# Query units in two token halves, an earlier search of the half tile, and gathered rows moved between stages of a product-key expert layer

## What is computed

```python
q = (tb @ w_q).reshape(PEER_BLOCK, PEER_HEADS, 2, PEER_HALF)      # 1024 -> 8 heads x 2 x 128
s = einsum('thik,hink->thin', q, sub_keys)                        # 128 keys per head and half
s_top, i_top = top_k(s, 16)
cand = s_top[:, :, 0, :, None] + s_top[:, :, 1, None, :]
best_s, best_c = top_k(cand.reshape(..., 256), 16)
eid = i1 * N_KEYS + i2                                            # one of 16384 experts
g = softmax(best_s)
act = gelu(einsum('thkd,td->thk', u_tab[eid], tb))
x = x + einsum('thkd,td', g * act, v_tab[eid])
```

## Time and profile before

| | us |
|---|---|
| median of 3 runs | 2277.96 |
| lowest and highest | 2274.05, 2281.59 |
| the profiled execution | 2277.83 |
| its span | 2276.1 |
| TensorE busy in it | 2229.8 (98%) |
| VectorE busy | 1585.5 (70%) |
| ScalarE busy | 814.1 (36%) |
| GpSimd busy | 1475.2 (65%) |

### The profile page before, as it was taken

The page is one execution under the profiler, slowest core; times in us unless marked ns, Lnnn a source line. Parts: engine busy times, 40 slices in busy tenths (PEclk is TensorE's granted clock), DMA queues, the critical chain, the costliest instruction groups (busy, mean ns, idle before and its releaser), DMA issues.

```text
span 2276.1 us, 38281 instructions
## 1 busy us (share of the span) xinstructions
PE 2229.8 (98%) x14510; PEld 2152.9 (95%) x14510; DVE 1585.5 (70%) x2800; ACT 814.1 (36%) x1201; POOL 1475.2 (65%) x851
## 2 busy tenths in 40 slices
PE   8999999999999999999999999999989999999998
PEld 8999999997799999999999999999989999999998
DVE  7866444546678336768978889898478777777774
ACT  4443223432133002133433344444344444444442
POOL 5554333432354555557878887889778888888873
PEclk9999999999999999999999999999999999999999
DMA  6224323225763233248888897999999999999982
GB/s 215 84 80 137 97 92 101 93 96 194 250 230 128 84 126 94 84 132 275 304 286 289 291 313 248 300 331 318 355 364 396 374 369 374 385 370 375 381 311 79
DMA packets 212800, 535.19 MB, mean 235 GB/s; under 512 B 16816, under 2 KB 101168, under 8 KB 210224
## 3 DMA queue, kind: packets, MB, share of 16 engines
q1 hardware_dynamic: 111392, 234.65, 31.7%
q0 software_dynamic: 46080, 167.79, 19.7%
q10 hardware_dynamic: 55184, 130.77, 15.7%
HBM read 453.89 MB, written 79.25 MB: 234 GB/s over the span
## 4 chain that ended last, share of the span: by engine, by line
PE 85%; DVE 7%; POOL 2%; DMA 2%; ACT 1%; issue 1%; ACTq 0%; DVEq 0%; SPq 0%; POOLq 0%
PE ps L1008 47%; PE ps L732 30%; PE ps L1066 2%; POOL w_lo L706 1%; DVE prev L1875 1%; PE ps L909 1%; DMA gbuf<-gate_scratch 1%; POOL ug L698 1%; PE ps L896 1%; PE ps L904 1%; PE ps L1021 1%; PE ps L913 1%; PE ps L929 1%; DVE n_lo L1991 1%; DVE oh L2097 1%
## 5 line engine op out<-in xcount | busy, mean ns | idle before, releaser
L673 POOL TENSOR_SCALAR w_hi<-raw 128x1024 fp32r<-128x1024 f32 x129 | 139.5, 1081 | 516.3 <-issue 384.0
L706 POOL TENSOR_TENSOR w_lo<-raw,e_hi 128x1024 fp32r<-128x1024 f32 x128 | 326.4, 2550 | 95.2 <-PE ps L1008 85.3
L706 POOL TENSOR_TENSOR w_lo<-raw,w_hi 128x1024 fp32r<-128x1024 f32 x128 | 318.9, 2492 | 86.6 <-PE ps L1008 84.5
L1008 PE MATMUL ps<-p_hi,w_lo 128*128 128x416 f32 x1024 | 361.4, 353 | 0.0
L1008 PE MATMUL ps<-g_hi,w_lo 128*128 128x416 f32 x1024 | 359.6, 351 | 0.0
L675 POOL TENSOR_TENSOR w_lo<-raw,w_hi 128x1024 fp32r<-128x1024 f32 x129 | 320.7, 2486 | 10.8
L732 PE MATMUL ps<-h_hi,w_hi 128*128 128x288 f32 (+2 forms) x1216 | 273.0, 306 | 1.6 <-ACT ma L1342 1.6
L732 PE MATMUL ps<-h_lo,w_hi 128*128 128x288 f32 (+2 forms) x1216 | 262.1, 297 | 0.0
L732 PE MATMUL ps<-h_hi,w_lo 128*128 128x288 f32 (+2 forms) x1216 | 261.7, 296 | 0.0
L2075 DVE CUSTOM_DVE_ANT_0 ug<-ug,ps 128x1024 f32<-128x1024 f32 x160 | 192.3, 1213 | 72.2 <-DMA ug<-rows_u,eid 56.4
L698 POOL DMA_INDIRECT ug<-rows_u,eid x160 | 214.8, 1342 | 37.5 <-issue 24.3
(11 more groups left out here) (358 smaller groups left out, 5086.0 us busy)
## 6 DMA issues: line engine op xcount, KB each, us to landing
raw<-units SPq DMA_DIRECT2D x385, 512.0 KB
gate_scratch<-gt SPq DMA_DIRECT2D x52, 512.0 KB
activation_scratch<-ge ACTq DMA_DIRECT2D x120, 208.0 KB
abuf<-activation_scratch ACTq DMA_DIRECT2D x30, 832.0 KB
gbuf<-gate_scratch ACTq DMA_DIRECT2D x30, 832.0 KB
prev<-ssm_in ACTq DMA_DIRECT2D x8, 1024.0 KB, 6.7
ssm_s<-prev ACTq DMA_DIRECT2D x8, 1024.0 KB, 4.5
cxb<-parked_tiles ACTq DMA_DIRECT2D x8, 870.0 KB, 6.8
```

What stands on the lines that cost most here:

```text
L673: pool.tensor_scalar(w_hi[:, s, :], raw[:, r, :], 1.0, 1.0, ALU.mult, ALU.mult).then_inc(s_whi, 1)
L706: pool.tensor_tensor(w_lo[:, n % 2, :], raw[:, n % RAW, :], e_hi[m % HS_].bitcast(F32), ALU.subtract)\
L1008: last = mm(accp[par], w[:, k * P:(k + 1) * P], x_[:, k, t0:t0 + ND], start=k == 0 and i == 0, stop=k == KT - 1 and i == 2)
```

## The change

- The query projection runs as 32 half units (N_HALF): the 16 weight units are streamed twice, first for tokens 288 to 575, then for tokens 0 to 287. High parts come from ScalarE and low parts from GpSimd, as for expert units; half units count as m = -32 to -1. Q_RAW becomes 8 half units.
- The first tile (128 gathered tokens) is searched in two parts of four heads, with scores before half units 10 and 17. The half tile's scores come before half unit 19, and it is searched second, from m = -5; the full tiles follow at 6, 28 and 50 instead of 4, 24 and 44.
- The first seven gathers stand behind the low parts of m = -13, -11, ... -1 instead of units 2, 3 and 4.
- Dots beside searches: 14 in the half tile and 38 in each full tile, all 128, instead of 26, 26, 26 and 12. Beside gate blocks, from the third on, 24 of the 32 spread dots, instead of 38 of the 128; the turned rows for them lie in PSUM banks 2 and 3. The last 8 spread dots come one a unit from unit 120 on; before, 32 stood there, 9 of them ahead of the gates.
- VectorE makes the wider sum `g_spread` ahead of the first gate block, not in the half tile's search. The gates of the first block start at unit 74 instead of 76.

```diff
-TT = [(T_ROWS, PH)] + [(t, PH) for t in range(0, T_HALF, P)] + [(T_HALF, PH // 2)]
+TT = [(T_ROWS, PH), (T_HALF, PH // 2)] + [(t, PH) for t in range(0, T_HALF, P)]
+DENSE = [j for j, (t, _) in enumerate(TT) if t < ND]
-PAIR = 2
+PAIR = 4
-UT = [4, 20, 20, 20, 10]
-M_TILE = [sum(UT[:j]) for j in range(len(UT) + 1)]
+M_TILE = [None, -5, 6, 28, 50, 72]
+UT = [0] + [b - a for a, b in zip(M_TILE[1:], M_TILE[2:])]
-UG_FIRST = [3, 2, 2]
-M_FIRST = 2
+M_FIRST = -13
+UG_FIRST = [1, 0, 1, 0, 1, 0, 1, 0, 1, 0, 1, 0, 1]
-DOTS_T = [0, 26, 26, 26, 12]
+DOTS_T = [0, 14, 38, 38, 38]
+N_BESIDE = 24
+B_SPREAD = 2
+DOTS_B = [0] * B_SPREAD + [(b + 1) * N_BESIDE // (NB - B_SPREAD) - b * N_BESIDE // (NB - B_SPREAD)
+                           for b in range(NB - B_SPREAD)]
+N_TAIL = N_PICK + N_BESIDE
-DOTS_U = [9, 0, 0, 1, 1, 1, 1, 1, 1]
-DOTS_V = [2, 2, 2, 2, 2, 2, 3, 2]
+DOTS_U = [0, 1, 1, 1, 1, 1, 1, 1, 1]
+DOTS_V = [0, 0, 0, 0, 0, 0, 0, 0]
-Q_RAW = 4
+Q_RAW = 8
+N_HALF = 2 * N_WQ
+U_PEER = U_WQ + N_HALF
...
-            for m in range(2 * NKEYS):
+            for m in range(-N_HALF, 2 * NKEYS):
                 n = U_PEER + m
-                pool.wait_ge(s_ehi, m + 1)
+                pool.wait_ge(s_ehi, N_HALF + m + 1)
                 pool.wait_ge(s_unit, n - 1)
...
+            query_half(0, gu, parts=s_u, ready=KT)
+            added_squares(1 + GROUPS)
+            query_half(1, gu, (0, 2))
+            last_squares(1 + GROUPS)
+            query_half(1, gu, (2, KT))
+            query_half(2, gu, (0, 4))
+            spread_out(1 + GROUPS)
+            query_half(2, gu, (4, KT))
+            for j in range(3, Q_RAW):
+                query_half(j, gu)
+            query_half(Q_RAW, (g_hi, g_lo), parts=s_h, ready=KT)
+            for j in range(Q_RAW + 1, N_HALF):
+                if j == Q_RAW + 2:
+                    first_scores(0)
+                elif j == Q_RAW + 4:
+                    turn_rows(0, g_sum[:], h_rows)
+                elif j == N_WQ + 1:
+                    first_scores(1)
+                elif j == N_WQ + 3:
+                    pe.wait_ge(s_scs, 1)
+                    scores(1)
+                query_half(j, (g_hi, g_lo))
...
+                if b == B_SPREAD - 1:
+                    pe.wait_ge(s_ud, N_PICK)
+                    turn_rows(1, spread_columns, h_beside)
...
+            for j in range(Q_RAW, N_HALF):
+                half = slice(HK, TK) if j < N_WQ else slice(0, HK)
+                link(query_copy(j, q[:, j % N_WQ, half]))
+                act.sem_inc(s_accf[(U_WQ - L_SHIFT + j) % 2], 1)
+                act.sem_inc(s_q, 1)
+                if j == N_HALF - HS_:
+                    act.wait_ge(s_qs, Q_RAW)
+                expert_hi(j + HS_ - N_HALF)
+                if j == Q_RAW + 2:
+                    first_scores_out(0)
+                elif j == N_WQ + 1:
+                    first_scores_out(1)
+                elif j == N_WQ + 2:
+                    first_exp(0)
+                elif j == N_WQ + 4:
+                    scores_out(1)
+                elif j == N_WQ + 9:
+                    first_exp(1)
```

More of the change, by code:

```diff
@@ L131, in dots_of, with turned_by @@
     return range(d0, d0 + DOTS_B[b])
-N_TURNED = len(TT) - 1 if ND > T_HALF else len(TT) - 2
+def turned_by(j):
+    return sum(i <= j for i in DENSE)
 def store_after(B, i):
@@ L965, in _, with expert_part, expert_unit, query_half @@
                 tile(U_WO + j, L_WO + j, m_hi, m_lo)
[L966 to L979, removed]
+            gu = (gu_hi, gu_lo)
+            L0 = U_PEER - L_SHIFT
+            def expert_part(m, c, half, out, mov, columns, ks=(0, KT), parts=None, ready=0):
+                par = (L0 + c) % 2
+                if ks[0] == 0:
+                    pe.wait_ge(s_w, U_PEER + 1 + m)
+                    pe.wait_ge(s_accf[par], half)
+                hi, lo = e_hi[c], w_lo[:, (U_PEER + c) % 2, :]
+                for k in range(*ks):
+                    if parts:
+                        pe.wait_ge(parts, ready + k + 1)
+                    for i, (w, x_) in enumerate(((hi, mov[0]), (hi, mov[1]), (lo, mov[0]))):
+                        last = mm(out, w[:, k * P:(k + 1) * P], x_[:, k, columns],
+                                  start=k == 0 and i == 0, stop=k == KT - 1 and i == 2)
+                if ks[1] == KT:
+                    last.then_inc(s_unit, 1)
+            def expert_unit(m, c, half, mov, t0, parts=None):
+                expert_part(m, c, half, accp[(L0 + c) % 2], mov, slice(t0, t0 + ND), parts=parts)
+            def query_half(j, mov, ks=(0, KT), parts=None, ready=0):
+                m = j - N_HALF
+                t0 = HK if j < N_WQ else 0
+                expert_part(m, m % HS_, (L0 + m) // 2, queried(j), mov, slice(t0, t0 + HK), ks, parts, ready)
             def first_scores(c):
@@ L2074, in row_dot @@
                 rows = row_landed(k)
-                dve.tensor_tensor_reduce(rows, rows, h_rows if k < N_PICK else h_spread, 1.0, 0.0, ALU.mult, ALU.add, dots[:, k:k + 1])\
+                dve.tensor_tensor_reduce(rows, rows, h_rows if k < N_PICK else h_beside if k < N_TAIL else h_spread, 1.0, 0.0, ALU.mult, ALU.add, dots[:, k:k + 1])\
                     .then_inc(s_ud, 1)
@@ L2190, in step @@
                         row_dot(due.pop(0))
-                search(PARTS + j, 0, heads, step, j - 1)
+                search(PARTS + j, 0, heads, step, turned_by(j - 1))
                 dve.sem_inc(s_pk, 1)
@@ L2334, in inputs_of @@
     units[U_WO:U_WQ] = tiles(A(w_o)[0])
-    units[U_WQ:U_PEER] = tiles(A(peer_w_q)[0])
+    units[U_WQ:U_WQ + N_WQ] = units[U_WQ + N_WQ:U_PEER] = tiles(A(peer_w_q)[0])
     uu = A(peer_u)[0].reshape(NKEYS, NKEYS, KT, P).transpose(1, 3, 2, 0).reshape(NG, GI, P, D)
```

201 lines of the change are left out of this document (91 added, 110 removed).

## The result

Measured: 2295.9 us, median of five runs (2294.1 to 2300.6), against 2278.4 us of the kernel before (2274.1 to 2281.8, five runs on the same chip). By the medians the change made the kernel 17.5 us slower. The ratio over all these runs is 1.0085, 95% interval 1.0073 to 1.0096, which is 19.4 us (17 to 22). The profiled execution took 2295.7 us, so its sum can be set against the 2277.8 of the one before.

The account below looks back on a forecast made before the run. TensorE was taken to bound the kernel, so only its waits could be won; terms 0.9 + 1.6 + 2.4 + 2.6 + 4.4 - 1.5 - 6.3 = +4.1 on 2277.8 gave 2281.9 us, range 2268 to 2296.

Parts of the forecast that it names:

- rival C: Tiles among expert units: GpSimd 96% full cannot catch up, each full search costs 6.6 us; 2290.3 us, chance 0.20.
- Step 1: Start of the query stage: fewer matmuls stand before the spreading of the inverse root, +1.6 us.
- Step 3: Query stage's second search: its comparison holds GpSimd's low parts and gathers beside half units, +2.6 us.
- The eight transposes: One more turning of rows, priced within the query projection, +0.9 us.
- Step 2: Near half unit 20: TensorE waits for a low part queued behind the gather that needs four heads' ids, +2.4 us.
- Step 5: Ends of the three full searches: late dots 5.4 us, then lock 3.0 each; 11.4 against 9.6 before, +1.8 us.
- Step 4: Expert units: bursts of four gathers behind units 0 and 37, +1.1 us each, and the half tile, +0.4.
- The gate blocks: 24 gathers instead of 38 there, so TensorE loses less to late low parts, -1.5 us.
- the turning: One more turning of rows as eight transposes, expected with the query projection, +0.9 us.
- Step 6: Last units before the outputs: fewer gathers precede the second group's gates' load, 12 us instead of 16.73; -6.3 us with clock.
- A: Searches among expert units: long steps fall between low parts and cost nothing; 2269.2 us, faster, chance 0.20.
- B: Last units: they give nothing back, the gates' loads take 16.7 us again; 2288.2 us, chance 0.16.

Follow-up runs that it names:

- e_mix: Changed kernel with comparison and product of the four later searches in halves, due dots taken between the halves; 2287.2 us, ratio 1.0042 to the kernel before.
- e_fill2: Changed kernel with unused matmuls filling TensorE's waits in the query stage and among expert units, also ahead of units 28 and 73; 2292.9 us, ratio 1.0063.
- e_nolock: Changed kernel with comparison and product of the three full searches replaced by instructions with one SBUF input; 2292.2 us, ratio 1.0055.
- e_tail: Changed kernel with no spread dot beside the gate blocks, all 32 at the end as in the kernel before; 2305.8 us, ratio 1.0118.
- e_even: Changed kernel with 32 dots a full tile instead of 38, the 18 others beside the first nine gate blocks; 2295.2 us, ratio 1.0065.
- b_split4: Kernel before with the searches among expert units cut in quarters, dots left where they were; 2276.8 us, ratio 0.9989.
- e_mix3: Changed kernel with quarters and dots between in the first two full searches, halves without dots between in the last; 2288.2 us, ratio 1.0045.
- b_mix4: Kernel before with comparison, product and sum of searches among expert units in quarters, due dots between; 2270.0 us, ratio 0.9954.

## Why the prediction was wrong, point by point

The forecast was 2281.9; it missed by 14.0 us. The direction was right. The measured time lies at the very top of the stated range, 2296, which was there for rival C. Of the miss 8.0 us are steps 4 and 5, 3.7 steps 1 to 3, and 3.9 lie ahead of the change; the rest takes some 2 off. Its own steps:

**Step 1** was too small. It took the spreading of the inverse root to stay where it was, 13.1 us after the stage's start, with 12 matmuls fewer before it. The spreading came after 15.4 us, and the missing matmuls still had to be done: 2.3 + 1.6 = +3.9 for +1.6. TensorE had waited 1.57 us in half unit 0 and then stood at 0.51 of its clock from 900 to 907 us. In e_mix, where the same wait was not followed by half clock, the spreading came after 12.3 us, and the step is worth +0.8. So half clock, which the step left out, made 3.1 of the 3.9.

**Step 3** held: the second search cost 2.8 us at half units 26 and 27, for +2.6. The eight transposes took 0.8, but among the gate blocks. What the sum left out in the stage's favour is a wait of 0.87 us for ScalarE at its end in the kernel before, which is gone.

**Step 2** had the wait right in its place (half unit 20, behind the gather that waits for its ids) and 0.9 short in size, 3.3 for 2.4. It left out what follows the wait, half clock from 978.7, worth 1.6.

**Step 5 failed**, and it is the largest part. It priced the three search ends at 11.4 us, 5.4 with late dots in the first tile and 3.0 of lock in each other. The waits came to 11.1 us, the stretches to 17.7: 6.8, 5.9 and 5.0. What is missing is the half clock behind each wait, 6.1 us, which the sum carried for the last units and nowhere else, though the earlier trace rows showed 0.91 at the middle search end of the kernel before. By e_fill2 half of those 6.1 would have been lost to the next wait anyway. That the waits agree with the 11.4 is in part luck. In the first tile the step had late dots hold unit 28 for 5.4 us; what came was 3.88 at unit 26, from a gather held by the comparison, which had to be out of the way before the late dots showed (e_nolock: 4.13). In the other two the lock held 4.05 and 3.19, for 3.0 each. And "nine slots let VectorE run 5 us ahead, which covers it" was not so: with the lock gone, e_nolock waited 2.86 us for dots in the second tile.

**Step 4** gave +1.1 for a burst of four gathers: 1.5 behind unit 37, nothing behind unit 0. The half tile's 0.4 was measured as 0.4.

**The gate blocks** gave -2.6 without the turning, for -1.5. The two waits of the kernel before (1.04 and 0.78 us) are gone. By e_tail 24 gathers cost nothing there, by e_even 18 more cost 0.31 us each. Ahead of them stood a wait that no step had: unit 73, 2.0 us, behind a gather of 3.01 and a low part of 3.70 us beside the one-hots of the first block, which now fall on a full tile's last gathers.

**Step 6** held in place and size: the first three output units took 6.8 us less (17.5 for 24.4), the gates' load 11.4 for 12, with 3 gathers in the 30 us ahead of it instead of 12. That the fewer gathers are the cause fits these rows and was not shown: e_tail, made for it, lost its time elsewhere.

**The unchanged stage**: 3.9 us of the 17.5 between the two executions lie ahead of the change, 2.9 of them in one stretch of half clock at 558.7. It stood in 7 of 17 profiled executions of the study, b_split4's among them, whose code is the kernel before's there. So it can come without the change. But that the change has no part in it is not shown: 13 of the 14 executions with the changed query stage had such a stretch somewhere between 530 and 620 us, and 1 of 3 of the kernel before and its two variants. The interval over all runs, 17 to 22 us, is the better measure of the whole, and how much of it these stretches make was not settled.

**The rivals.** A fell: each full search cost time. B fell: the gates' load took 11.4 us, not 16.7. C is not settled. Its 6.6 us a search end are near the measured 5.9 on average, in part for another reason (the clock), and the lighter load of e_even took 3.6 and 2.5 us off the first two ends and nothing off the third. None had the clock.

**What the change costs once the search ends are eased in both**: e_mix3 against b_mix4, by the two ratios 1.0045 and 0.9954, is still about 21 us; between their own executions it is 22.2: 5.0 ahead of the change, 10.4 in the query stage, 12.7 from unit 0 to the gates, where nine waits of 0.3 to 1.8 us for low parts remain, and -6 behind. So the search ends, the largest wrong term of the sum, are not by themselves the reason for the loss: the kernel before has them too, and loses 9.9 us by them. How the 12.7 divide between the fuller queue of GpSimd and its meetings with VectorE stays open; e_even changed both at once.

## What to carry to other kernels

When a wait of TensorE is priced, price the clock behind it too, and then take off what the late engine would have caught up in that time: here one half was left. When an engine does long instructions beside a queue that must not stop, look for two limits behind each other, what the instruction holds and what it postpones, and ease both: pieces with the due work between them took ten microseconds out of the kernel before, pieces alone four. Do it only where that engine has time; ahead of a stage that waits for its result the same pieces cost as much as they save.

## What the runs showed of the hardware

A gather by GpSimd took 4.43 us when it met VectorE's comparison, and 0.94 when an instruction of the same length with one SBUF input ran there. By the Trainium skill, "SBUF — State Buffer", section "Who interferes with whom", a VectorE instruction with two SBUF inputs contends with GpSimd's reads of SBUF, but does not stall the preparing of a DMA (the page calls the reason inferred). Here a gather was delayed by 3.5 us, and the measurement decides. The gather also reads the row numbers (`eid`) that GpSimd needs, so the runs do not tell whether it was that read or the preparing of the transfers that was held.

Short waits were enough for half clock, and not surely. The same wait of 1.5 to 1.6 us at half unit 0 was followed by it in 9 of 14 executions and not in 5; the wait of 3.3 at half unit 20 in 7 of 9. The executions of one kernel lay up to 12 us apart (e_mix, 2280.5 to 2293.0), and this is a part of it.
